# Two-layer hybrid decoder trunk, one core: the mixing projection as seven block products instead of eight column units

## The reference, cut to what matters

```python
q_i, k_i, w_i ...                                  # index scores choose 256 keys per query
out_a = _dsa_attention(q_a, k_a, v_a, q_i, k_i, w_i)
out_b = _rms_norm(_diff_attention(q_b, k_b, v_b, lam), diff_norm_g[l]) * (1.0 - lam_init)
mixed = jnp.concatenate([out_a.reshape(b, s, -1), out_b.reshape(b, s, -1)], axis=-1)
h = h + mixed @ w_out[l]
h = h + _memory_attention(_rms_norm(h, mem_attn_norm_g[l]), ...)
h = h + _conv_glu(_rms_norm(h, ffn_norm_g[l]), ...)
```

## Time and profile before

| | |
|---|---|
| median of three runs | 3075.44 us |
| the profiled execution | 3077.7 us, span 3075.9 us |
| granted TensorE clock, mean | 0.991 of full |
| TensorE matmul busy | 2955.4 us, 96% of the span |
| VectorE, ScalarE, GpSimd busy | 71%, 48%, 23% |
| matmuls | 14940 |
| moved by DMA | 350.32 MB, 114 GB/s on average |

### The profile page before, as it was taken

One profiled execution on the slowest core, in us unless ns is written; L12 is line 12 of the kernel. 1 busy time (PEld: TensorE's weight loads), 2 busy tenths in 40 slices (PEclk: granted clock), 3 DMA queues, 4 the chain that ended last, 5 costly groups with the idle time before them and its releaser, 6 DMA issues. The chain is left out here.

```text
span 3075.9 us, 40324 instructions
## 1 busy us (share of the span) xinstructions
PE 2955.4 (96%) x14940; PEld 2453.7 (80%) x14940; DVE 2197.4 (71%) x3590; ACT 1478.5 (48%) x2469; POOL 708.6 (23%) x390
## 2 busy tenths in 40 slices
PE   8998889999999999999999989899999999999998
PEld 6797876788877888888877978668888788888877
DVE  7778887343469999988548688763443899998783
ACT  6378766433353333344325787663343533334442
POOL 1121036221221222201222200652213222222021
PEclk9999999999999999999999999999999999999999
DMA  7555730432342222264355477104416222224542
GB/s 235 172 145 141 156 101 18 136 130 76 77 94 83 82 83 83 82 223 140 113 136 145 112 181 157 45 27 154 138 41 137 55 83 83 83 85 151 168 131 75
DMA packets 314050, 350.32 MB, mean 114 GB/s; under 512 B 21872, under 2 KB 244592, under 8 KB 313344
## 3 DMA queue, kind: packets, MB, share of 16 engines
q1 hardware_dynamic: 298912, 314.20, 35.3%
q0 software_dynamic: 6656, 16.78, 2.9%
q10 hardware_dynamic: 8288, 16.78, 1.7%
HBM read 270.04 MB, written 111.21 MB: 124 GB/s over the span
## 5 line engine op out<-in xcount | busy, mean ns | idle before, releaser
L1033 POOL TENSOR_TENSOR w_lo<-raw,w_hi 128x1024 fp32r<-128x1024 f32 (+4 forms) x124 | 268.0, 2167 | 831.1 <-ACT w_hi L1123 829.5
L2438 PE MATMUL ps<-xs_hi,w_hi 128*128 128x512 f32 (+2 forms) x1328 | 412.0, 391 | 12.6 <-ACT relu_b L1338 6.2
L2438 PE MATMUL ps<-xs_lo,w_hi 128*128 128x512 f32 (+2 forms) x1328 | 410.4, 390 | 0.0
L2438 PE MATMUL ps<-xs_hi,w_lo 128*128 128x512 f32 (+2 forms) x1328 | 409.8, 390 | 0.0
L2438 PEld LDWEIGHTS ps<-xs_hi,w_hi 128*128 128x128 f32 (+2 forms) x1328 | 246.1, 187 | 71.6 <-ACT relu_b L1338 7.6
L2438 PEld LDWEIGHTS ps<-xs_lo,w_hi 128*128 128x128 f32 (+2 forms) x1328 | 248.3, 187 | 54.1
L2438 PEld LDWEIGHTS ps<-xs_hi,w_lo 128*128 128x128 f32 (+2 forms) x1328 | 248.3, 187 | 54.2
L1077 POOL TENSOR_SCALAR p_a<-p_a,rca 128x1024 f32<-128x1024 f32 (+7 forms) x96 | 179.0, 1874 | 402.8 <-DVE rca L2062 402.6
L2728 PE MATMUL ps<-xs_hi,w_hi 128*128 128x512 f32 x672 | 262.7, 391 | 7.8 <-DVE w_lo L2282 4.4
L2729 PE MATMUL ps<-xs_lo,w_hi 128*128 128x512 f32 x672 | 262.2, 390 | 0.0
L2730 PE MATMUL ps<-xs_hi,w_lo 128*128 128x512 f32 x672 | 262.1, 390 | 0.0
(11 more groups left out here) (380 smaller groups left out, 6866.8 us busy)
## 6 DMA issues: line engine op xcount, KB each, us to landing
raw<-in_w_gu SPq DMA_DIRECT2D x48, 512.0 KB, 4.6
act_spill<-cv SPq DMA_DIRECT2D x44, 512.0 KB, 5.9
raw<-in_w_in SPq DMA_DIRECT2D x32, 512.0 KB, 5.8
qk_spill<-t_hi SPq DMA_DIRECT2D x24, 512.0 KB, 3.4
qk_spill<-t_lo SPq DMA_DIRECT2D x24, 512.0 KB, 3.6
k_b<-qk_spill SPq DMA_DIRECT2D x32, 384.0 KB
gate_e<-in_w_gu SPq DMA_DIRECT2D x20, 512.0 KB, 4.0
up_e<-in_w_gu SPq DMA_DIRECT2D x20, 512.0 KB, 5.3
```

What stands on the lines that cost most here:

```text
L1033: nc.gpsimd.tensor_tensor(w_lo[s][:, w], raw[s][:, w], w_hi[s][:, w].bitcast(f32), ALU.subtract).then_inc(lo_done, 1)
L2438: ins = M(dst[0:c, a:b], w[s][:, k * c:(k + 1) * c], xt[:, a:b], start=(at == 0 and w is w_hi and part == 0), stop=(at == kc - 1 and w is ...
```

## The change

The 1024 x 1024 by 1024 x 1024 product is cut into two-by-two blocks of 512, and seven block products take the place of eight (the same tables as in the down projection). A product p has four steps n = 4p + j, one per 128 input features; a step has 12 matmuls of 128x512 (four column blocks, three each), and a unit is now two steps: 14 units of 24 matmuls per layer for 8 of 48. The blocks of `w_out` that are sums (products 0, 1, 4, 5) are made in DRAM during the input projection: SyncE copies (`rows_o`, `cols_o`) at four units, GpSimd issues adding DMAs at four later ones. The weights of product 6 are a difference that GpSimd makes in place (`out_difference`). Products 2 to 6 need sums of blocks of `mixed`: GpSimd makes those of products 2, 3 and 6, VectorE those of 4 and 5, each four steps ahead, into the slot that the step four before has left. ScalarE rounds each, VectorE makes the low part. VectorE adds the seven products to four quadrants of the residual, 20 additions of 128x1024. The first unit of the next projection (`qm 0`) takes half-chunks: first the eight whose quadrants are done early (`EARLY`), then eight (`LATE`). The squares of the norm move behind `qm 0` and `qm 1`. And in the index stage ScalarE's split of `kb 2` moves behind the relus of block 6.

```diff
-    u += [("out", m, KC, P) for m in range(KC)]
+    u += [("out", m, KC, P) for m in range(2 * NPR)]
...
+KO = KC // 2
+SQUARES_AT = {0: [2, 3, 4], 1: [5, 6, 7]}
+NO = NPR * KO
+BY_POOL = (2, 3, 6)
+OUT_POOL = [n for n in range(2 * KO, NO) if n // KO in BY_POOL]
+OUT_DVE = [n for n in range(2 * KO, NO) if n // KO not in BY_POOL]
+EARLY = [(k, int(k < KO)) for k in range(KC)]
+LATE = [(k, int(k >= KO)) for k in (0, 1, 4, 5, 2, 3, 6, 7)]
+COPY_AT = {("rb", 1): 0, ("qb", 0): 1, ("qb", 1): 2, ("qb", 2): 3}
+ADD_AT = {("vb", (0, 0)): 0, ("vb", (0, 1)): 1, ("vb", (1, 0)): 2, ("vb", (1, 1)): 3}
...
-    j += [("unit", U_AT["out", m]) for m in range(KC)]
+    j += [("O", p, i) for p in range(NPR) for i in range(2)]
...
-MEMORY = [("qm", 0), ("ssqc", 1), ("qm", 1), ("qm", 2), ("SM", 0), ("qm", 3), ("qm", 4), ("SM", 1), ("qm", 5), ("qm", 6), ("qm", 7)]
+MEMORY = [("qm", 0), ("qm", 1), ("qm", 2), ("ssqc", 1), ("SM", 0), ("qm", 3), ("qm", 4), ("SM", 1), ("qm", 5), ("qm", 6), ("qm", 7)]
...
+        out_acc = at("out_acc", [P, 2, KO, HALF], f32, AB)
...
+        rows_o = nc.dram_tensor("rows_o", (DEPTH, KO * P, D), f32, kind="Internal").ap()
+        cols_o = nc.dram_tensor("cols_o", (DEPTH, KC * P, HALF), f32, kind="Internal").ap()
...
+        def out_block(part, n):
+            return (xs_hi, xs_lo, xs_raw)[part][:, KO + n % KO, HALF:T]
...
+            def copy_out_weights(m):
+                l, r, c = now["layer"], slice(P * m, P * m + P), slice(2 * P * m, 2 * P * m + 2 * P)
+                sp.dma_start(rows_o[l, r, :], w_out[l, r, :]).then_inc(pre_copy, 16)
+                sp.dma_start(cols_o[l, c, :], w_out[l, c, 0:HALF]).then_inc(pre_copy, 16)
+            def load_out_weights(u, s):
+                l, (p, jj) = now["layer"], divmod(u, 2)
+                r0, r1 = slice(2 * P * jj, 2 * P * jj + 2 * P), slice(P * KO + 2 * P * jj, P * KO + 2 * P * jj + 2 * P)
+                left, right = slice(0, HALF), slice(HALF, D)
+                src = (rows_o[l, r0, left], rows_o[l, r0, right], w_out[l, r0, left], w_out[l, r1, right],
+                       cols_o[l, r0, :], cols_o[l, r1, :], w_out[l, r0, left])[p]
+                if u == 0:
+                    after_out(sp, pre_sum, 16 * 2 * KO)
+                sp.dma_start(raw[s][:, :].rearrange("p (k c) -> p k c", c=HALF), src.rearrange("(k p) c -> p k c", p=P)).then_inc(w_dma[s], 16)
+                if p == NPR - 1:
+                    wait_full(sp, ("VA", 0))
+                    sp.dma_start(out_second(u), w_out[l, r1, right].rearrange("(k p) c -> p k c", p=P)).then_inc(d2_dma[u % 2], 16)
...
+            def sum_out_weights(m):
+                l, r, c = now["layer"], slice(P * m, P * m + P), slice(2 * P * m, 2 * P * m + 2 * P)
+                if m == 0:
+                    after_out(pool, pre_copy, 16 * 2 * KO)
+                pool.dma_start(rows_o[l, r, :], w_out[l, P * (KO + m):P * (KO + m + 1), :], accum_op=ALU.add, max_dma_last_dim=4096).then_inc(pre_sum, 16)
+                pool.dma_start(cols_o[l, c, :], w_out[l, c, HALF:D], accum_op=ALU.add, max_dma_last_dim=4096).then_inc(pre_sum, 16)
+            def out_sum(n):
+                if n not in OUT_POOL:
+                    return
+                (b0, b1, sign), j = DN_PRODUCTS[n // KO], n % KO
+                wait_out(pool, n - KO)
+                nc.gpsimd.tensor_tensor(out_block(2, n), mixed_block(b0, j), mixed_block(b1, j),
+                                        ALU.add if sign > 0 else ALU.subtract).then_inc(sum_pool, 1)
+            def out_difference(g, u):
...
+                block = raw[s][:, :].rearrange("p (k c) -> p k c", c=HALF)
+                nc.gpsimd.tensor_tensor(block, block, out_second(u), ALU.subtract).then_inc(ddiff_done, 1)
...
+                    kind, i = UNITS[n % U][0:2]
                     split_lo(l * U + n)
+                    if kind == "out" and 2 * NPR - 3 <= i < 2 * NPR - 1:
+                        out_difference(l * U + n + 1, i + 1)
+                    if kind == "out" and i:
+                        out_sum(2 * i + 2)
+                        out_sum(2 * i + 3)
+                    if (kind, i) in ADD_AT:
+                        sum_out_weights(ADD_AT[kind, i])
...
-                    seen = index_relus(I_BLOCKS.get(n - 1, [])[:1], seen)
+                    seen = index_relus(I_BLOCKS.get(n - 1, []), seen)
                     if n == VW_AFTER + 1:
                         split_hi(n + 1)
-                    seen = index_relus(I_BLOCKS.get(n - 1, [])[1:], seen)
...
+                            for n in range(KO):
+                                A(out_block(0, n), out_source(n), ACT.Copy).then_inc(xhi_done, 1)
...
+                def out_hi(n):
+                    if n >= NO:
+                        return
...
+                    A(out_block(0, n), out_source(n), ACT.Copy).then_inc(xhi_done, 1)
...
+                for i, (ks, t) in enumerate(late):
+                    act.dma_start(out_acc[:, i, :, :], h_spill[ks, :, t].rearrange("k p t -> p k t")).then_inc(back_dma[0], 16)
+                for ks, t in early:
+                    act.dma_start(xs_raw[:, ks, t], h_spill[ks, :, t].rearrange("k p t -> p k t")).then_inc(back_dma[1], 16)
...
+                for n in range(NO):
+                    if n and n % 2 == 0:
+                        split_hi(U_AT["out", n // 2] + 1)
+                    out_hi(n + KO)
+                    if n == 8:
+                        memory_high(0)
+                    if n in (17, 21):
...
+                        ks, t = early[i]
+                        act.dma_start(h_spill[ks, :, t].rearrange("k p t -> p k t"), xs_raw[:, ks, t]).then_inc(back_dma[1], 16)
+                    if n >= 24:
+                        for b in EARLY[2 * (n - 24):2 * (n - 24) + 2]:
+                            early_high(b)
+                after_out(act, sum_pool, len(OUT_POOL))
+                after_out(act, dsum_done, len(OUT_DVE))
+                for ks, t in early:
+                    act.dma_start(h_t[:, ks, t], h_spill[ks, :, t].rearrange("k p t -> p k t")).then_inc(back_dma[0], 16)
+                wait_full(act, ("O", NPR - 1, 1))
+                for at, b in enumerate(LATE):
+                    if at % KO == 0:
+                        wait_drained(act, ("O", NPR - 1, at // KO))
+                    A(half_of(xs_hi, b), half_of(h_t, b), ACT.Copy, scale=packs[:, l, G_MQ + b[0]:G_MQ + b[0] + 1]).then_inc(xhi_done, 1)
+                split_hi(U_AT["qm", 1])
...
+                def out_lo(n):
+                    if n >= NO:
+                        return
+                    after(dve, xhi_done, X_OUT + n + 1)
+                    V.tensor_tensor(out_block(1, n), out_source(n), out_block(0, n).bitcast(f32), ALU.subtract).then_inc(xlo_done, 1)
+                def out_add(p, at):
+                    adds = DN_ADDS[p]
+                    if at >= 2 * len(adds):
+                        return
+                    i, (row, col, sign) = at // len(adds), adds[at % len(adds)]
+                    job = ("O", p, i)
+                    wait_full(dve, job)
+                    if p:
+                        wait_drained(dve, ("O", p - 1, i))
...
+                    ins = V.tensor_tensor(new, old, bank(job)[:, :].rearrange("p (c t) -> p c t", t=HALF), ALU.add if sign > 0 else ALU.subtract)
+                    if at % len(adds) == len(adds) - 1:
+                        ins.then_inc(drained_of(job), 1)
...
+                for n in range(NO):
+                    if n >= KO and n % KO < 2:
+                        for at in range(2 * (n % KO), 2 * (n % KO) + 2):
+                            out_add(n // KO - 1, at)
+                    out_sum(n + KO)
+                    out_lo(n + KO)
+                    if n in (9, 10):
+                        memory_low(0, 4 * (n - 9))
+                    if n >= 24:
+                        for at in range(2 * (n - 24), 2 * (n - 24) + 2):
+                            half_low(EARLY[at], at, xs_raw)
+                for at in range(3):
+                    out_add(NPR - 1, at)
+                for at in range(KO):
+                    half_low(LATE[at], KC + at, h_t)
+                out_add(NPR - 1, 3)
+                for at in range(KO, KC):
+                    half_low(LATE[at], KC + at, h_t)
...
-                for m in range(KC):
-                    project(U_AT["out", m], ready=(lambda k: after(pe, xlo_done, KC + k + 1)) if m == 0 else None, order=OUT_ORDER if m == 0 else None,
-                            chunk_read=out_read if m == KC - 1 else None)
+                for n in range(NO):
+                    p, j = divmod(n, KO)
+                    g = l * U + U_AT["out", n // 2]
+                    if j == 0:
+                        sets = [claim(("O", p, i)) for i in range(2)]
+                    wait_lows(pe, g, n % 2)
+                    after(pe, xlo_done, X_OUT + n + 1)
+                    x_hi, x_lo = out_block(0, n), out_block(1, n)
+                    for i in range(4):
```

(8 more changed lines are left out.)

200 lines of the change are left out of this document (135 added, 65 removed).

## The result

Forecast 3092 us; measured **3109.3 us** in the median of four runs (3104.3 to 3113.6) against 3075.6 for the kernel before: **1.0102 times the time before (95% interval 1.0087 to 1.0117)**. The direction was right; the 16 us I had summed are 34. The profiled execution took 3111.8 us.

What follows compares the result with a forecast made beforehand. TensorE's matmuls were taken to bound the kernel; -21.8 - 2.8 + 43.0 - 2.2 = +16.2 us, added to the median 3075.44, gave 3092 us. The forecast's own range was 3083 to 3101, the wider one 3064 to 3104.

Steps and rivals of the forecast that it cites:

- (1) start: Output projection's start: unit 1's load lands at 572.6, its split ends after TensorE's first unit; +0.9 us per layer.
- (2) products 2 and 3: Units 4 to 7: GpSimd rounds of 7.45 us against units of 5.44, plus memory-key work, less margin; +9.5 us per layer.
- products 4 and 5: Taken at nothing: VectorE makes the sums, and GpSimd's two parts (2.56 us) leave room.
- (3) product 6: Units 12 and 13: GpSimd also makes the weight difference, rounds of 9.9 us, 4.5 too long, twice; +8.1 us per layer.
- (4) end: After the last output matmul: VectorE's low parts and additions come late for the next projection; +3.0 us per layer.
- The saved matmuls: Output projection: seven products for eight units, -10.88 us per layer, -21.8 in all.
- the old waits: Output projection: TensorE's two old waits go with ScalarE's chain of `h_t` loads before unit 2; -2.8 us.
- Index split: Index stage: the relu of block 6, moved ahead of a split, ends sooner, -1.5 us; layer 1's 0.67 wait goes; -2.2.
- Weight sums in DRAM: Input projection: SyncE's copies and GpSimd's adding DMAs fall where there is room; taken at zero, 0 to +2 allowed.
- Rival B: Output projection: the rounds hold but the new GpSimd and VectorE pairs do not take turns; 3075 us, no change; chance 0.15.
- Rival A: Output projection: only GpSimd and VectorE's shared turn counts, 82.6 us against 76.2 of matmuls; 3063 us, faster; chance 0.14.
- Rival C: Output projection: the weight loads bind too, 28.3 us per layer; 3105 us; chance 0.13 for C and above.

Runs made afterwards that it cites:

- split first: The changed kernel with ScalarE's split of the next weights put before the rounding of the unit's second operand instead of behind it; ratio 1.0082.
- memory keys later: Changed kernel with memory loads issued late, weight split before second rounding, and memory-key rounding moved from step 8 to 15, low parts to 16 and 18; ratio 1.0041.
- the four kernels with the long wait: Four variants of the changed kernel giving VectorE operand sums or product 6's weight differences that GpSimd had; ratios 1.0124, 1.0062, 1.0043, 1.0065; each waits 7.33 us in layer 1's index stage.
- the kernel with idles: The kernel before, with GpSimd repeating a low weight part at four output-projection units so that TensorE idles once for each; 3107.1 us in one execution.

## Why the prediction was wrong

The terms of the sum are delays, what a part adds to TensorE's list. The trace gives the same thing: the time from one unit's first matmul to the next one's, less 24 matmuls of 0.227 us, holds the waits, the restarts and the slow matmuls together. By that measure, for layers 0 and 1:

| term | forecast, us per layer | measured |
|---|---|---|
| (1) start | +0.9 | 9.1 and 7.9 |
| (2) products 2 and 3 | +9.5 | 9.3 and 8.0 |
| products 4 and 5 | 0 | 0.0 and 0.9 |
| (3) product 6 | +8.1 | 6.8 and 6.6 |
| (4) end | +3.0 | 3.9 and 5.4 |
| together, with 0.1 in product 0 | 21.5 | 29.3 and 29.1 |

- **The step that failed** is term (1), the start, +0.9. I followed the weight load of unit 1, and TensorE did not wait for that unit at all. It waited 5.95 and 5.53 us for unit 2, whose split stood in ScalarE's list behind two DMA issues that held it 9.59 and 9.27 us; with the restart and the slow matmuls that is 9.1 and 7.9. Moving the two issues took 6.5 and 6.7 us off the stretch and left it 9.8 and 10.1 us over the kernel before. My sum for a layer was 21.5 - 10.9 - 1.4 = 9.2. So with that one step put right the forecast stands within 1 us per layer.
- **A price that no term held** is the half clock, 5.6 and 4.8 us of slow matmuls. At the start it is part of the 9.1 and 7.9. In the rounds it took the place of waits. Its sign was there to see: the mean granted clock of 0.991 in my own table says that something lowers it somewhere, and I did not look at what stands before those places.
- The kernel before also holds ScalarE for 15 us at this place, but by another thing: six loads wait for each other there by semaphore, and each issue takes 0.33 us. The old wait of 1.8 us came of it. It does not show that an issue can be held.
- **The saved matmuls** (-21.8) and the old waits (-2.8): as forecast.
- **(2) Products 2 and 3**: the mechanism was right (split first, memory keys later and the rounds show all three parts: GpSimd's own work, ScalarE's answer, VectorE's two-input operations). That its size came out near is in part luck: the slow matmuls that I did not have stand in it, and the first round, 6.4 us, had no turn.
- **(3) Product 6**: rounds of 8.7 us where I took 9.9; GpSimd's operations ran undisturbed there (2.39, 2.53, 2.50).
- **(4) The end**: 1.9 us of it is a wait, with its restart, that I did not foresee, for the weights of `qm 1`, whose split stands behind the late roundings.
- **Index split**, -2.2: nothing, by the run that undoes it. I took VectorE's first sum as fixed at 101.43; it waits for a DMA and moves, and a turn with GpSimd took the rest.
- **Weight sums in DRAM**, 0: no effect that can be measured.
- **In all**, the delays were 7.8 and 7.6 us too small, the index split 2.2 too hopeful, and the rest of the span added 1.0: that is the 18 us that are missing, within 1. The measured 3109.3 us lies above the whole range of 3064 to 3104. Of the signs that I had named, the matmuls and the 20 us of waits came; but the stage took 101 us and not 94 to 98, and the longest wait was at unit 2, which I had not named.
- **Rival B** (the new pairs do not take turns) is refuted: `xs_lo` of 128x512 takes 0.92 us in the mean against 0.69 alone, and a single one of the same size 2.41 beside GpSimd. **Rival A**'s 3063 us did not come, and whether its count of the two engines' shared work is a floor no run shows: the stretch reached 247.1 us at best, where the count would give some 239; the kernel before has 245.0. **Rival C** named 3105 us, nearest of all, for another reason: TensorE's waits lead back to GpSimd, VectorE and the held issues, not to late weights. The text says that the range takes in C, but it ends at 3104.

No kernel beat the one before; the best, memory keys later, is 0.41% slower. What stays open is why the turns with GpSimd fall otherwise in the four kernels with the long wait.

## What to carry to other kernels

First ask whether another engine's round sets the pace of TensorE. If not, as in the kernel with idles, a wait costs its length, a restart (0.27 us here) and the half-clock stretch behind it (2.6 to 2.8 us here when TensorE idled for 6 us or more). If a round does, the length of the round is the price and the slow matmuls are inside it. Read DMA issues as instructions of the engine that issues them, and follow that engine's list, not only the load: when many megabytes went out at once, whatever stood behind the last issue waited. And where two engines and a rounding engine feed each other in a ring, moving one operation moves the wait; what took time off was order (what stands ahead of the answer that someone waits for).

## What the runs showed of the hardware

- Issuing two 1 MB loads from ScalarE took 9.59 us (3.70 and 5.86) right behind four others on its queue, 0.37 us each when spread, and 0.36 and 0.58 from SyncE at the same moment. The Trainium skill (page "DMA: Bandwidth & Descriptors", section "Issuing engines are not separate DMA queues") calls the time on the sequencer that an issue takes "usually small relative to the DMA itself"; here the held issues took about a quarter and a third of the 16 us that their loads took to land, and they stopped the compute instructions behind them.
- A 512 KB load behind 2 MB on its queue landed after 16 us, and after 7.7 (unit 3 in the change) with DMA as busy but those 2 MB on the other engine's queue.
- The half-clock stretch was 13 to 14 matmuls behind idles of 6.24 and 12.81 us alike, and between 6 and 14 behind the waits of 4.5 to 8.8 us at units 2 and 3 of all these kernels. Waits of 1.8 to 3.5 us, in a row with others, had 7 or 8 behind them in some places and none in others, and a single one of 2.36 none.
- Every VectorE instruction that took over 1.5 us more than its like (24 in the change, 22 to 28 in each of the other kernels) started while a GpSimd operation ran and ended up to 1.1 us after it, one of 128x6 with 2.37 us for 0.16 among them.
